# Rounds of a top-k selection and half a rotation moved between stages of a hybrid attention/SSM trunk

## The chip, the cores and the metric

One core of a Trainium2 chip runs the whole kernel in one launch. The metric is device time in microseconds (us). The engines are TensorE (matrix products), VectorE (element-wise work, DVE in the rows), ScalarE (activations, ACT), GpSimd (POOL) and SyncE, which issues most DMAs (SP). Each engine runs its own queue in order and meets the others through semaphores.

## The reference

Two layers of a streaming-encoder trunk over 512 tokens of width 1024. Each is a half-step FFN, a mixer of two parallel head groups, and another half-step FFN, with RMS norms and gates from a conditioning vector; a last norm follows. In the mixer, one projection gives queries q (8 heads of 64), one shared key k and value v, an indexer (4 heads qi, one key ki, weights wi) and the input of a state-space model (SSM). The part that matters here is the sparse attention, for each block of 128 queries:

```python
q = apply_partial_rope(q); k = ...; qi = ...; ki = ...     # rotary: t*cos + swapped(t)*sin
rel = relu(einsum('bqhd,bsd->bqhs', qi, ki))
score = einsum('bqhs,bqh->bqs', rel, wi) * idx_scale
score = where(key_chunk <= q_chunk, score, -inf)
vals, idx = top_k(score, 128)                              # topk = min(256, 512 // 4)
logits = einsum('bqhd,bqkd->bqhk', q, k[idx]) * att_scale  # -inf where vals is not finite
out = softmax(logits) @ v[idx]
```

The SSM's output passes a GELU and a gated linear unit (GLU), both groups are normed, and `w_out` projects them.

## The kernel before

Features lie on partitions, tokens along the free dimension. Every large product is split in three: an operand is a high and a low part (`w_hi`, `w_lo`, `h_hi`, `h_lo`), ScalarE makes the high part of each streamed weight tile (`split_hi`, L698), VectorE the low one (`split_lo`, L1003), and TensorE runs three matmuls (`split3`, L1706 to L1708). Each engine's order is written out by hand in its own function; there is no planner.

**The mixer.** First come twelve projection tiles, t = 0 to 11 (`project(t)` on TensorE). Between them lie rotations, the SSM's states, and, at t = 8, 9, 10, the indexer for query blocks 1, 2, 3: a product on TensorE, a rectifier on ScalarE (L873), a weighted accumulation on VectorE (`index_acc`, L1371 and L1373) into `score[b]`, whose width is 128 (b + 1): 256, 384 and 512. Block 0 needs no selection.

**Selection.** The 128 largest of each row are found in 16 rounds of 8 for each block: `topk_max` (L1385) finds the 8 largest, `topk_take` (L1391, a value load and a replacement) overwrites them with a marker. Each waits for the one before it on the same block. `topk_end` (L1396) makes the mask out of the markers.

**Head steps.** Then come 32 steps e, four blocks of eight heads. Step e: TensorE makes the logits of head e + 1 (L1990), VectorE adds the mask to those of head e and finds the row's extreme (`mask_head`, L1415), ScalarE exponentiates into `tmp_b` (`p_exps`, L888), TensorE transposes (`turn`, L2000), ScalarE copies (`p_copy`, L897), and TensorE multiplies the values of head e - 1 (L2009). Logits of e wait for the mask step of e - 2. `TOPK_WITH[e]` names the blocks whose rounds run at step e: before, blocks 1 and 2 at steps 0 to 7, blocks 2 and 3 at 8 to 15, block 3 at 16 to 23. The other rounds of block 1 are in the tiles: two beside the indexer at t = 9, four at t = 10, two at t = 11. The norm of block b - 1 runs in parts at fixed steps of block b (`att_step`, whose first part, L1425 and L1426, divides by the row sums; L903, GpSimd's L1673, L1438, L908 and L1443 follow). From step 10 TensorE also does the GLU, two tiles k at a step (`GLU_AT`), and from step 18 three matmuls at a step whose result nobody uses (`keep_streaming`, L2017). VectorE does the gate (L1531), ScalarE the tanh and the squares (L956, L963), and two splits of late weight tiles follow ScalarE's at steps 1 and 2.

**Rotations.** Eight tiles are rotated (r = 0 to 7; r = 4 to 7 are the queries, each for two heads): TensorE multiplies by a swap matrix (L1970), VectorE forms tile times cosine (L1357), swapped tile times sine (L1358) and their sum (L1359). Only the last, r = 7, is shared with GpSimd: VectorE makes the sine product at step 4 (L1527), GpSimd the cosine product (L1623) and the sum (L1626) in `last_rope`, behind the low parts of the SSM output (`y_low`, L1618). Logits of head 4 need r = 6, those of head 6 need r = 7.

Of the kernel before, what the change touches and what calls it, by code (L numbers as in the profile page):

```python
# [23 lines left out]
ALU = mybir.AluOpType  # L24
# [9 lines left out]
QB = SEQ // P  # L34
F = 2816
FT = F // P
HEADS = 8
HD = 64
AT = HEADS * HD // P
# [74 lines left out]
INDEX_FROM = 8  # L114
SUM_BEHIND = 2
KEEP_FROM = 18
TOPK_WITH = [(1, 2)] * HEADS + [(2, 3)] * HEADS + [(3,)] * HEADS + [()] * HEADS
OUT_SPLIT_AT = {0: 14, 1: 15, 19: 16, 23: 17, 25: 18, 27: 19}
PREP = {}
for m in range(4):  # L120
    for i in range(4):
        PREP[4 * m + i + 1] = (m, i)
DVE_STEPS, POOL_STEPS = 273, 86
SMALL = 72


# [65 lines left out]
def trunk(nc, a):  # L192
    ctx = ExitStack()
    with ctx:
# [3 lines left out]
        def sem(name):  # L198
            return ctx.enter_context(nc.semaphore(name))
# [176 lines left out]
        z_copy = Signal(sem("z_copy"), 12)  # L376
        swap_mm = Signal(sem("swap_mm"), 8)
        rope_done = Signal(sem("rope_done"), 8)
        last_sin = Signal(sem("last_sin"), 1)
        last_cos = Signal(sem("last_cos"), 1)  # L380
        v_tr = Signal(sem("v_tr"), 1)
        v_done = Signal(sem("v_done"), 2)
        idx_mm = Signal(sem("idx_mm"), 12)
# [308 lines left out]
        def _(act):  # L692
# [150 lines left out]
            def mixer_act(l):  # L843
# [84 lines left out]
                for t in range(12):  # L928
# [13 lines left out]
                    if t == 10:  # L942
                        for m in GELU_AT[t]:
                            gelu(m)
                act.wait_ge(*h_done.at(l, 2 * KT - 1))
                for e in range(NA):
                    b, h = e // HEADS, e % HEADS
                    p_exps(e)
                    for m in GELU_HI_AT.get(e, ()):
                        gelu_high(m)  # L950
                    if e in TANH_AT:
                        n = TANH_AT[e]
                        used(act, l, m0 + 12 + n)
                        if n >= 2:
                            act.wait_ge(*ssm_y.at(l, n - 2))
                        nc.scalar.activation(glu_t[:, n % 2, :], ps[:, 4 + n % 2, :], ACT.Tanh, scale=0.5,  # L956
                                             bias=half_bias[:, n:n + 1]).then_inc(glu_act.sem, 1)
                    if e in SQUARE_AT:
                        n = SQUARE_AT[e]
                        act.wait_ge(*ssm_y.at(l, n))  # L960
                        if n >= 2:
                            act.wait_ge(*ssm_ss.at(l, n - 2))
                        nc.scalar.activation(sq_t[:, n % 2, :], ssm_t[:, n, :], ACT.Square).then_inc(ssm_sq.sem, 1)  # L963
                    for n in SSM_HI_AT.get(e, ()):
                        act.wait_ge(*ssm_f.at(l, n))
                        nc.scalar.activation(h_hi[:, AT + n, :].rearrange("p (j t) -> p j t", t=L),
                                             ssm_t[:, n, :].rearrange("p (t j) -> p j t", t=L), ACT.Copy).then_inc(ssm_hi.sem, 1)
                    p_copy(e)
                    if e in OUT_SPLIT_AT:
                        split_hi(l, m0 + OUT_SPLIT_AT[e])  # L970
                    if b and h == 2:
                        att_square(b - 1)
                    if b and h == 7:
                        att_high(b - 1)
# [21 lines left out]
        def _(dve):  # L996
# [351 lines left out]
            def mixer_dve(l, step):  # L1348
                m0 = MIX_BASE

                def rope(r):
# [7 lines left out]
                    V.tensor_tensor(dst, part[:, 0, :], part[:, 1, :], ALU.add).then_inc(rope_done.sem, 1)  # L1359
                    dve.wait_ge(*rope_done.at(l, r))  # L1360

                def index_acc(n):

                    b, h = n // IDX_HEADS + 1, n % IDX_HEADS
                    w = (b + 1) * P
                    dve.wait_ge(*idx_relu.at(l, n))
                    if n:
                        dve.wait_ge(*idx_acc.at(l, n - 1))
                    dst, w_h = score[b], wi_n[:, b, h:h + 1]
                    if h == 0:  # L1370
                        i = V.tensor_scalar(dst, tmp_a[:, n % 2, 0:w], w_h, None, ALU.mult)  # L1371
                    else:
                        i = V.scalar_tensor_tensor(out=dst, in0=tmp_a[:, n % 2, 0:w], scalar=w_h, in1=dst, op0=ALU.mult, op1=ALU.add)  # L1373
                    i.then_inc(idx_acc.sem, 1)
# [111 lines left out]
                for t in range(2, 12):  # L1486
                    split_lo(l, m0 + t + AHEAD)
                    if t in (10, 11):
                        for _ in range(2):
                            topk_max(1)  # L1490
                            topk_take(1)
                    for r in ROPE_SLOT.get(t, ()):
                        rope(r)
                    if t == 3:
                        mask0()
                        step(V.memset(hs[:], 0.0), V.memset(dec[:, :, 0:1], 0.0))
                    if t in STATES_AT:
                        s5_scan(STATES_AT[t])
                    if INDEX_FROM <= t < INDEX_FROM + 3:
                        if t == INDEX_FROM:  # L1500
                            dve.wait_ge(*v_done.at(l, 1))
                        for n in range(IDX_HEADS):
                            index_acc((t - INDEX_FROM) * IDX_HEADS + n)
                            if t > INDEX_FROM:
                                (topk_max, topk_take)[n % 2](1)
                        topk_start(t - INDEX_FROM + 1)
                for e in range(NA):
                    b, h = e // HEADS, e % HEADS
                    blocks = TOPK_WITH[e]
                    if blocks:  # L1510
                        topk_max(blocks[0])
                    mask_head(e)
                    if len(blocks) > 1:
                        topk_max(blocks[1])
                    if blocks:
                        topk_take(blocks[0])
                    if b:
                        att_step(b - 1, h)
                    if b > 1 and h == 0:
                        att_step(b - 2, 8)  # L1520
                    if len(blocks) > 1:
                        topk_take(blocks[1])
                    if blocks and h == HEADS - 1:
                        topk_end(blocks[0])
                    if e == LAST_ROPE:
                        dve.wait_ge(*swap_mm.at(l, 7))
                        V.tensor_tensor(ssm_t[:, 1, :], ps[:, ROPE_BANKS[7][1], :], rope_s[:], ALU.mult).then_inc(last_sin.sem, 1)  # L1527
                    if e in GATE_AT:
                        n = GATE_AT[e]
                        dve.wait_ge(*glu_act.at(l, n))  # L1530
                        V.scalar_tensor_tensor(out=ssm_t[:, n, :], in0=glu_t[:, n % 2, :], scalar=1.0,  # L1531
                                               in1=u_t[:, n].rearrange("p a b -> p (a b)"), op0=ALU.add, op1=ALU.mult).then_inc(ssm_y.sem, 1)
                    if e - 1 in OUT_SPLIT_AT:
                        split_lo(l, m0 + OUT_SPLIT_AT[e - 1])
                    if e == ROOT_AT:
                        dve.wait_ge(*ssm_ss.at(l, ST - 1))
                        rms(l, 2, 4 * SW, step)
                    for n in SSM_AT.get(e, ()):
                        if n == 0:
                            dve.wait_ge(*bcast.at(l, 2))  # L1540
                        V.scalar_tensor_tensor(out=ssm_t[:, n, :], in0=ssm_t[:, n, :], scalar=half_gain[:, n:n + 1],
                                               in1=ps[:, 6, :], op0=ALU.mult, op1=ALU.mult).then_inc(ssm_f.sem, 1)
                    for n in SSM_LO_AT.get(e, ()):
                        dve.wait_ge(*ssm_hi.at(l, n))
                        V.tensor_tensor(h_lo[:, AT + n, :].rearrange("p (j t) -> p j t", t=L),
                                        ssm_t[:, n, :].rearrange("p (t j) -> p j t", t=L),
                                        h_hi[:, AT + n, :].bitcast(F32).rearrange("p (j t) -> p j t", t=L), ALU.subtract).then_inc(mix_done.sem, 1)
# [52 lines left out]
        def _(pool):  # L1600
# [16 lines left out]
                pool.wait_ge(*y_hi.at(l, m))  # L1617
                Q.tensor_tensor(h_lo[:, AT + m, :], u_t[:, m].rearrange("p a b -> p (a b)"), h_hi[:, AT + m, :].bitcast(F32), ALU.subtract).then_inc(y_done.sem, 1)  # L1618

            def last_rope(l):  # L1620

                pool.wait_ge(*z_copy.at(l, ROPE_TILE[7]))
                Q.tensor_tensor(ssm_t[:, 0, :], z_t[:, ROPE_TILE[7] % 2, :], rope_c[:], ALU.mult).then_inc(last_cos.sem, 1)  # L1623
                pool.wait_ge(*last_cos.at(l, 0))
                pool.wait_ge(*last_sin.at(l, 0))
                Q.tensor_tensor(q_t[:, AT - 1, :], ssm_t[:, 0, :], ssm_t[:, 1, :], ALU.add).then_inc(rope_done.sem, 1)  # L1626

            def ready(l, event, step):

# [38 lines left out]
            for l in range(DEPTH):  # L1668
# [14 lines left out]
                Q.memset(toep[:, 3], 0.0).then_inc(toep0.sem, 1)  # L1683
                s5_rot(l, step)
                power(l, 1)
                for m in range(ST):
                    y_low(l, m)
                last_rope(l)
                for b in range(2):
                    att_power(b)  # L1690
                power(l, 2)
# [485 lines left out]
```

## Time and profile before

| | us |
|---|---|
| median of 3 runs | 2104.31 (2103.47 to 2107.48) |
| the profiled execution | 2102.22 |
| its span | 2100.4 |
| TensorE busy | 2023.8 (96%) |
| VectorE busy | 1317.9 (63%) |
| ScalarE busy | 693.9 (33%) |
| GpSimd busy | 260.1 (12%) |

The span runs from the first to the last instruction of one profiled execution. Busy time is a sum over stages with different limits, so a stage has to be read by itself: the head steps of layer 0 lie between about 550 and 652 us, those of layer 1 between about 1574 and 1676.

### The profile page before, as it was taken

To read this page: it belongs to the slowest core of one execution; us is meant where nothing else is said; L and a number is where in the kernel's file an instruction comes from. 1 tells how busy PE (TensorE), PEld (TensorE's weight loads), DVE (VectorE), ACT (ScalarE), POOL (GpSimd) and SP (SyncE) were. 2 spreads that over 40 slices of the span, in tenths; PEclk is the share of its full clock that TensorE was granted. 3 is DMA by queue.
4 is the path that set the end of the run, shared out by engine and by line. 5 is a ranking of instruction groups with operands and counts; after the bars stand their busy time and mean duration, and the time that the engine had idled before them with its cause. 6 is when DMAs were issued, how large, how long until landed. Compare 5 with 4: busy or idle time off the path is not lost.

```text
span 2100.4 us, 25289 instructions
## 1 busy us (share of the span) xinstructions
PE 2023.8 (96%) x9548; PEld 1632.4 (78%) x9548; DVE 1317.9 (63%) x2057; ACT 693.9 (33%) x1061; POOL 260.1 (12%) x231
## 2 busy tenths in 40 slices
PE   6999899999899999999999999999998999999998
PEld 5788678877577788888878877888775787888886
DVE  6778856566884764543467697375779656545334
ACT  4332222341444422222342322233334534223223
POOL 0006900400100000000000295040001000000000
PEclk8999999999799999999999999999997999999999
DMA  8465556343101454433347365444320135463332
GB/s 290 124 212 186 157 155 183 86 109 94 56 20 52 135 172 145 158 103 92 89 139 222 121 185 152 152 146 112 100 70 22 41 89 172 120 193 115 104 93 78
DMA packets 395985, 264.77 MB, mean 126 GB/s; under 512 B 56560, under 2 KB 371672, under 8 KB 395864
## 3 DMA queue, kind: packets, MB, share of 16 engines
q1 hardware_dynamic: 387360, 260.94, 41.1%
q10 hardware_dynamic: 8504, 2.22, 0.5%
q8 instruction: 76, 1.25, 0.2%
q14 instruction: 45, 0.37, 0.1%
HBM read 254.98 MB, written 6.29 MB: 124 GB/s over the span
## 4 chain that ended last, share of the span: by engine, by line
PE 65%; issue 21%; DVE 9%; ACT 3%; DMA 1%; SPq 0%; POOL 0%; ACTq 0%; DVEq 0%; POOLq 0%
PE ps L1706 19%; PE ps L1707 18%; PE ps L1708 18%; DVE w_lo L1003 2%; DVE mod_acc L1024 2%; PE ps L1990 2%; PE ps L2009 1%; DVE h_lo L1084 1%; PE ps L1934 1%; PE ps L2017 1%; PE ps L2000 1%; PE ps L2082 1%; DMA stage<-in_ffn_w 1%; PE ps L2087 1%; PE ps L1970 1%
## 5 line engine op out<-in xcount | busy, mean ns | idle before, releaser
L1706 PE MATMUL ps<-h_hi,w_hi 128*128 128x512 f32 x1728 | 686.0, 397 | 22.1 <-DVE w_lo L1003 19.3
L1707 PE MATMUL ps<-h_lo,w_hi 128*128 128x512 f32 x1728 | 677.7, 392 | 0.0
L1708 PE MATMUL ps<-h_hi,w_lo 128*128 128x512 f32 x1728 | 677.1, 392 | 0.0
L1003 DVE TENSOR_TENSOR w_lo<-stage,w_hi 128x1024 fp32r<-128x1024 f32 (+2 forms) x322 | 394.1, 1246 | 164.4 <-ACT w_hi L698 162.1
L1706 PEld LDWEIGHTS ps<-h_hi,w_hi 128*128 128x128 f32 x1728 | 327.1, 189 | 103.7 <-DVE w_lo L1003 21.9
L1708 PEld LDWEIGHTS ps<-h_hi,w_lo 128*128 128x128 f32 x1728 | 327.1, 189 | 69.7
L1707 PEld LDWEIGHTS ps<-h_lo,w_hi 128*128 128x128 f32 x1728 | 327.0, 189 | 65.5 <-issue 0.5
L698 ACT ACTIVATE w_hi<-stage 128x1024 fp32r<-128x1024 f32 (+2 forms) x322 | 318.9, 1016 | 172.3 <-PE ps L1708 165.1
L1706 PE MATMUL ps<-g_hi,w_hi 128*128 128x512 f32 x704 | 276.7, 393 | 1.1 <-DVE g_lo L1318 1.1
L1707 PE MATMUL ps<-g_lo,w_hi 128*128 128x512 f32 x704 | 274.2, 389 | 0.0
L1708 PE MATMUL ps<-g_hi,w_lo 128*128 128x512 f32 x704 | 274.2, 389 | 0.0
L817 ACT ACTIVATE tmp_a<-ps 128x512 f32<-128x512 f32 x84 | 50.2, 597 | 494.9 <-PE ps L1708 494.8
L1316 DVE TENSOR_TENSOR tmp_b<-tmp_a,ps 128x512 f32<-128x512 f32 x84 | 57.5, 684 | 244.5 <-ACT tmp_a L817 242.2
L1024 DVE SCALAR_TENSOR_TENSOR mod_acc<-mod_stage,c_silu,mod_acc 128x1024 f32<-128x1024 f32 x126 | 187.2, 1485 | 8.5
L1109 DVE SCALAR_TENSOR_TENSOR x<-ps,gate,x 128x512 f32<-128x512 f32 x112 | 84.0, 750 | 152.8 <-PE ps L1708 152.8
L1706 PEld LDWEIGHTS ps<-g_hi,w_hi 128*128 128x128 f32 x704 | 132.2, 188 | 30.4 <-DVE g_lo L1318 1.8
L1708 PEld LDWEIGHTS ps<-g_hi,w_lo 128*128 128x128 f32 x704 | 132.1, 188 | 27.9
L1707 PEld LDWEIGHTS ps<-g_lo,w_hi 128*128 128x128 f32 x704 | 132.2, 188 | 26.8
L1606 POOL TENSOR_TENSOR small<-small 128x4 f32<-128x4 f32 x9 | 12.9, 1437 | 976.2 <-DVE small L1043 976.2
L821 ACT ACTIVATE g_hi<-tmp_b 128x512 fp32r<-128x512 f32 x88 | 55.6, 632 | 173.8 <-DVE tmp_b L1316 170.2
L1318 DVE TENSOR_TENSOR g_lo<-tmp_b,g_hi 128x512 fp32r<-128x512 f32 x84 | 67.8, 807 | 58.9 <-ACT g_hi L821 58.9
L1990 PE MATMUL ps<-k_t,q_t 64*128 64x128 f32 (+3 forms) x128 | 58.3, 550 | 3.2 <-POOL q_t L1626 3.2
(304 smaller groups left out, 1790.6 us busy)
## 6 DMA issues: line engine op xcount, KB each, us to landing
stage<-in_ffn_w SPq DMA_DIRECT2D x210, 512.0 KB, 4.7
mod_stage<-in_mod_w SPq DMA_DIRECT2D x144, 512.0 KB, 5.6
stage<-in_ffn_w SPq DMA_DIRECT2D x64, 448.0 KB, 4.0
stage<-in_w_in SPq DMA_DIRECT2D x20, 512.0 KB, 3.8
mod_first<-in_mod_w SPq DMA_DIRECT2D x16, 512.0 KB, 9.4
stage<-in_w_out SPq DMA_DIRECT2D x16, 512.0 KB, 4.1
x_in<-in_x SPq DMA_DIRECT2D x4, 512.0 KB, 5.1
stage<-in_w_in SPq DMA_DIRECT2D x8, 256.0 KB, 3.7
```

Of the source, the lines that this page charges most:

```text
L698: nc.scalar.activation(w_hi[:, c % RING, 0:n], stage[:, c % RING, 0:n], ACT.Copy).then_inc(w_split_hi.sem, 1)
L817: nc.scalar.activation(tmp_a[:, f % 2, :], ps[:, 2 * (f % 2), :], ACT.Silu).then_inc(silu_done.sem, 1)
L821: nc.scalar.activation(g_hi[:, f - FIRST_TILE[p], :], tmp_b[:, f % 2, :], ACT.Copy).then_inc(g_hi_done.sem, 1)
L1003: V.tensor_tensor(w_lo[:, c % RING, 0:n], stage[:, c % RING, 0:n], w_hi[:, c % RING, 0:n].bitcast(F32), ALU.subtract).then_inc(w_split_lo. ...
L1024: i = V.scalar_tensor_tensor(out=mod_acc[:], in0=chunk, scalar=c_silu[:, k:k + 1], in1=mod_acc[:], op0=ALU.mult, op1=ALU.add)
L1109: V.scalar_tensor_tensor(out=x[:, n, :], in0=ps[:, bank, :], scalar=gate[:, k3, n:n + 1], in1=x[:, n, :], op0=ALU.mult, op1=ALU.add).then_ ...
L1316: V.tensor_tensor(tmp_b[:, f % 2, :], tmp_a[:, f % 2, :], ps[:, 2 * (f % 2) + 1, :], ALU.mult).then_inc(g_full.sem, 1)
L1318: V.tensor_tensor(g_lo[:, f - FIRST_TILE[p], :], tmp_b[:, f % 2, :], g_hi[:, f - FIRST_TILE[p], :].bitcast(F32), ALU.subtract).then_inc(g_ ...
L1706: mm(out, hi, rhs_hi, start=first, stop=False)
L1707: mm(out, hi, rhs_lo, start=False, stop=False)
L1708: return mm(out, lo, rhs_hi, start=False, stop=last)
L1990: mm(ps[:, e % 2, 0:(b + 1) * P], q_t[r, h // 2, b * P:(b + 1) * P], k_t[r, 0:(b + 1) * P], start=True, stop=True).then_inc(logit.sem, 1)
```

## The change

Three rounds of block 1 leave steps 5 to 7 for t = 11, ahead of the rotation there. Three rounds of block 3 leave steps 13 to 15 for steps 16 to 18, which then have two each. Rotation 6 is divided as rotation 7 was: VectorE keeps the sine product, GpSimd makes the cosine product into `tmp_b` and adds. Since the exponentials write `tmp_b` too, ScalarE waits for that addition before step 0.

```diff
-TOPK_WITH = [(1, 2)] * HEADS + [(2, 3)] * HEADS + [(3,)] * HEADS + [()] * HEADS
+TOPK_WITH = [(1, 2)] * 5 + [(2,)] * 3 + [(2, 3)] * 5 + [(2,)] * 3 + [(3,)] * HEADS + [()] * HEADS
+TOPK_MORE = (16, 17, 18)
...
                 act.wait_ge(*h_done.at(l, 2 * KT - 1))
+                act.wait_ge(*rope_done.at(l, 6))
                 for e in range(NA):
...
+                def rope_sin(r):
+                    dve.wait_ge(*swap_mm.at(l, r))
+                    if r == 7:
+                        dve.wait_ge(*rope_done.at(l, 6))
+                    V.tensor_tensor((tmp_b if r == 6 else ssm_t)[:, 1, :], ps[:, ROPE_BANKS[r][1], :], rope_s[:], ALU.mult).then_inc(last_sin.sem, 1)
...
                     if t in (10, 11):
-                        for _ in range(2):
+                        for _ in range(2 if t == 10 else 5):
                             topk_max(1)
                             topk_take(1)
                     for r in ROPE_SLOT.get(t, ()):
-                        rope(r)
+                        (rope if r < 6 else rope_sin)(r)
...
                     if len(blocks) > 1:
                         topk_take(blocks[1])
-                    if blocks and h == HEADS - 1:
-                        topk_end(blocks[0])
+                    if e in TOPK_MORE:
+                        topk_max(3)
+                        topk_take(3)
+                    if h == HEADS - 1 and b + 1 < QB:
+                        topk_end(b + 1)
                     if e == LAST_ROPE:
-                        dve.wait_ge(*swap_mm.at(l, 7))
-                        V.tensor_tensor(ssm_t[:, 1, :], ps[:, ROPE_BANKS[7][1], :], rope_s[:], ALU.mult).then_inc(last_sin.sem, 1)
+                        rope_sin(7)
...
+            def rope_add(l, r):
+                pool.wait_ge(*z_copy.at(l, ROPE_TILE[r]))
+                pool.wait_ge(*rope_done.at(l, r - 1))
+                part = tmp_b if r == 6 else ssm_t
+                Q.tensor_tensor(part[:, 0, :], z_t[:, ROPE_TILE[r] % 2, :], rope_c[:], ALU.mult).then_inc(last_cos.sem, 1)
+                pool.wait_ge(*last_cos.at(l, r - 6))
+                pool.wait_ge(*last_sin.at(l, r - 6))
+                Q.tensor_tensor(q_t[:, r - 4, :], part[:, 0, :], part[:, 1, :], ALU.add).then_inc(rope_done.sem, 1)
...
                 power(l, 1)
+                rope_add(l, 6)
                 for m in range(ST):
                     y_low(l, m)
-                last_rope(l)
+                rope_add(l, 7)
```

## Rows read from the trace of the kernel before

**Rows 1.** Windows of layer 0's head steps: blocks 0, 1 and 2.

```profile
core 0: us, PE busy (x) PEld busy (x) DVE busy (x) ACT busy (x) POOL busy (x), PEclk, DMA share, GB/s
550.00:571.00 21.00, 13.43 (x43) 8.91 (x42) 20.18 (x73) 9.74 (x31) 8.37 (x6) 0.61 0.23 70
571.00:597.00 26.00, 24.50 (x103) 17.27 (x102) 24.47 (x74) 9.59 (x30) 0.56 (x1) 0.79 0.00 1
597.00:621.00 24.00, 24.00 (x140) 18.17 (x140) 19.68 (x51) 12.73 (x32) 1.95 (x2) 1.00 0.08 23
```

**Rows 2.** TensorE's waits, 577 to 640 us, all: total us, times, longest.

```profile
PE ps L2009 <- DVE ki_t L1426: 0.7, 1, 0.7
```

**Rows 3.** Timeline of VectorE, last projection tile: start, length, instruction, [idle before].

```profile
547.53 0.69 DVE L1003 TENSOR_TENSOR w_lo<-stage,w_hi 128x512 fp32r<-128x512 f32 x1 [1.21 <-ACT w_hi L698]
548.14 0.42 DVE L1385 MAX8 small<-score 128x8 f32<-128x256 f32 x1
...
549.34 0.43 DVE L1385 MAX8 small<-score 128x8 f32<-128x256 f32 x1
...
550.32 0.68 DVE L1357 TENSOR_TENSOR tmp_b<-z_t,rope_c 128x512 f32<-128x512 f32 x1
550.92 0.68 DVE L1358 TENSOR_TENSOR tmp_b<-ps,rope_s 128x512 f32<-128x512 f32 x1
...
552.50 0.43 DVE L1385 MAX8 small<-score 128x8 f32<-128x256 f32 x1 [0.17 <-DVE q_t L1359]
```

**Rows 4.** Timeline of VectorE, split of tile 14 and step 4.

```profile
556.75 0.69 DVE L1003 TENSOR_TENSOR w_lo<-stage,w_hi 128x512 fp32r<-128x512 f32 x1 [0.32 <-ACT w_hi L698]
...
562.19 0.41 DVE L1385 MAX8 small<-score 128x8 f32<-128x256 f32 x1
562.52 0.27 DVE L1415 CUSTOM_DVE_ANT_0 tmp_a<-ps,score 128x128 f32<-128x128 f32 x1
...
563.20 0.07 DVE L1391 MATCH_VALUE_LOAD score<-small,score 128x8 f32 x1
...
563.58 0.07 DVE L1391 MATCH_VALUE_LOAD score<-small,score 128x8 f32 x1
...
564.11 0.68 DVE L1527 TENSOR_TENSOR ssm_t<-ps,rope_s 128x512 f32<-128x512 f32 x1
```

**Rows 5.** Timeline of GpSimd, the sum of rotation 7.

```profile
564.93 1.26 POOL L1626 TENSOR_TENSOR q_t<-ssm_t 128x512 f32<-128x512 f32 x1 [2.23 <-DVE ssm_t L1527]
```

**Rows 6.** Timeline of ScalarE, last rectifier and first exponential's table load.

```profile
543.91 0.60 ACT L873 ACTIVATE tmp_a<-ps 128x512 f32<-128x512 f32 x1 [0.16 <-DVE score L1373]
...
553.21 1.28 ACT L888 ACT_TABLE_LOAD   x1 [3.31 <-DVE small L1415]
```

**Rows 7.** Timeline of TensorE: logits of 6 and 8, first GLU matmul, turn 19.

```profile
566.34 0.77 PE L1990 MATMUL ps<-k_t,q_t 64*128 64x128 f32 x2 [1.58 <-POOL q_t L1626]
...
569.22 1.22 PE L1990 MATMUL ps<-k_t,q_t 64*128 64x256 f32 x2
...
578.82 0.79 PE L1706 MATMUL ps<-h_hi,w_hi 128*128 128x512 f32 x1
...
609.80 0.49 PE L2000 MATMUL ps<-ident,tmp_b 128*128 128x128 f32 x3
```

**Rows 8.** Timeline of VectorE, the mask of step 8 and parts of step 16.

```profile
571.55 0.41 DVE L1415 CUSTOM_DVE_ANT_0 tmp_a<-ps,score 128x256 f32<-128x256 f32 x1
...
596.79 0.68 DVE L1385 MAX8 small<-score 128x8 f32<-128x512 f32 x1
597.39 0.53 DVE L1415 CUSTOM_DVE_ANT_0 tmp_a<-ps,score 128x384 f32<-128x384 f32 x1
...
597.93 0.67 DVE L1391 MATCH_REPLACE8 score<-small,score 128x512 f32<-128x512 f32 x1
```

**Rows 9.** Timeline of VectorE, two indexer accumulations and the split of tile 15.

```profile
542.34 0.49 DVE L1371 TENSOR_SCALAR score<-tmp_a,wi_n 128x512 f32<-128x512 f32 x1
...
543.08 0.73 DVE L1373 SCALAR_TENSOR_TENSOR score<-tmp_a,wi_n,score 128x512 f32<-128x512 f32 x1
...
559.28 1.06 DVE L1003 TENSOR_TENSOR w_lo<-stage,w_hi 128x512 fp32r<-128x512 f32 x1
```

More of the change, by code:

```diff
@@ L122 @@
         PREP[4 * m + i + 1] = (m, i)
-DVE_STEPS, POOL_STEPS = 273, 86
+DVE_STEPS, POOL_STEPS = 271, 86
 SMALL = 72
@@ L378, in trunk @@
         rope_done = Signal(sem("rope_done"), 8)
-        last_sin = Signal(sem("last_sin"), 1)
-        last_cos = Signal(sem("last_cos"), 1)
+        last_sin = Signal(sem("last_sin"), 2)
+        last_cos = Signal(sem("last_cos"), 2)
         v_tr = Signal(sem("v_tr"), 1)
@@ L1618, in y_low @@
                 Q.tensor_tensor(h_lo[:, AT + m, :], u_t[:, m].rearrange("p a b -> p (a b)"), h_hi[:, AT + m, :].bitcast(F32), ALU.subtract).then_inc(y_done.sem, 1)
[L1620 to L1626, printed above, removed]
+            def rope_add(l, r):
[6 more added lines that the diff above has]
+                Q.tensor_tensor(q_t[:, r - 4, :], part[:, 0, :], part[:, 1, :], ALU.add).then_inc(rope_done.sem, 1)
             def ready(l, event, step):
```

## The prediction

> **What bounds the kernel now.** The page's engine table shows TensorE busiest by far, but the change touches only some 70 us of each layer, so I read that stretch by windows [rows 1]. It has three regimes. In the first (heads 0 to 7 of attention block 0) VectorE is busy 20.18 of 21.00 us and TensorE 13.43. In the second (block 1) both are near full. In the third (block 2) TensorE is busy 24.00 of 24.00 and VectorE 19.68. The waits settle who sets the pace: from 577 to 640 us TensorE waits once, 0.7 us, at its start [rows 2]. It runs head steps, GLU matmuls and streaming matmuls end to end, so **from step 10 TensorE is the bound**, and whatever VectorE saves or spends there counts only where a turn (transpose) of probabilities comes late. Before step 10 VectorE sets the pace, helped by ScalarE's exponentials. I work the sum in layer 0 and double it: layer 1 shows the same waits and durations, moved by 1023.9 us.
>
> **The change, part by part.** All times of layer 0.
>
> *Last projection tile.* VectorE gets the split of tile 13 at 547.53, after a wait on ScalarE, and then runs two rounds of block 1. Alone, a round is a chain: 548.14 to 549.34 is 1.20 us [rows 3], because each half needs the other's result. They ended just as the swapped tile for rotation 6 was there, so their slot is full already. Three rounds more cost 3 x 1.20 = 3.6 us, with no idle time to take them. The rotation shrinks from three operations (550.32 to 552.50, with a short wait: 2.18 us) to one, 0.60 from start to start (the step from its first operation to its second). So step 0 begins at 552.50 + 3.6 - 1.58 = 554.52, **+2.0 us**.
>
> *The new wait on ScalarE.* The exponentials write the scratch in which GpSimd now adds rotation 6, so head 0's exponential, its table load and everything behind them on ScalarE wait for that addition: the two high parts of the SSM output, the probability copy and the split of tile 14, for which VectorE waits, and TensorE's first turn. VectorE's sine product would end at 553.92 + 0.68 = 554.60; GpSimd starts 0.14 after such an end and takes 1.27 (564.11 + 0.68 to 564.93) [rows 4, 5], and who waits for it starts 0.14 after its end (TensorE, 566.34 [rows 7]): ScalarE at 556.15, where it began its table load at 553.21 [rows 6]. ScalarE is **2.9 us** late. VectorE, 2.0 late, meets it at the split of tile 14 (0.32 idle today [rows 4]) and is 2.9 late from there to step 5. The cosine product costs nothing on this path: it needs only tile 10 and rotation 5, there by 542.3, and GpSimd has nothing to do then.
>
> *Steps 5 to 7* lose block 1's round. A step with both blocks is 1.92 (562.19 to 564.11 [rows 4]), of which block 1 is 0.33 from its maximum to the mask and 0.38 from its load to the other's (563.20 to 563.58), 0.72 unrounded. The full gain would be 2.2, but the remaining block's round is a chain of about 1.5 (0.55 maximum, 0.14 gap, mask beside it, 0.07 load, 0.54 replace, 0.13), so at most 3 x 0.43 = 1.3 is there. It also meets the other ring: head 6 waits for rotation 7 on GpSimd (1.58 on TensorE [rows 7]), 2.9 late like all of it; then TensorE, at its lower clock, needs logits, turn and values twice. Carried on from its rows: logits of 6 at 569.28, of 7 at 570.70, of 8 at 572.16, ready 1.22 + 0.22 later, at 573.60. Head 8's mask stood at 571.55 [rows 8]. **Net at block 1's start +2.05**; VectorE's own chain would give +1.7, no catching up +2.9. Steps 8 to 12 are unchanged and carry the delay into the GLU at step 10 (578.82 [rows 7]), where TensorE is the bound and it can't be made up.
>
> *Steps 13 to 15* lose block 3's round, 0.60 for the maximum (596.79 to 597.39) and 0.67 for the replacement [rows 8], 1.27 us each on VectorE. I count that as 0 for the time: TensorE waits there neither for VectorE nor for an exponential [rows 2]. It only builds a lead, and the lead is cut: step 16's last part waits for block 0's high part, made after TensorE's turn of 15 (to 597.8).
>
> *Steps 16 to 18* each get a second round of block 3, in chain with the first. By 0.69 + 0.14 + 0.08 + 0.68 + 0.13 a 512-wide round is 1.7 us. In the frame of before: step 16 ends at 600.06, step 17 masks at 600.8 and ends at 604.9 with its division and gate, step 18 masks at 605.5 and ends at 608.5, step 19 masks at 609.3. Exponential 18 just makes its turn; 19 ends at 610.6, and its turn stood at 609.80 [rows 7]. **+0.8** (0 if VectorE packs tighter by half a microsecond a step, 1.5 if looser). Steps 20 to 23 have slack to take the rest, with TensorE pacing.
>
> *A collision on GpSimd.* The cosine product would run from about 542.45 to 543.7, beside the second indexer accumulation of block 3. Today such a meeting shows once: the 512-wide split at 559.28 took 1.06 beside GpSimd's low parts, against 0.69 at 547.53 [rows 3, 9], so 0.37 more. The accumulation at 543.08 releases ScalarE's last rectifier at 543.91 [rows 6, 9], and behind that stand the GELU and the split for which VectorE waits until 547.53. Bounds: 0, if they don't meet, and 0.63, if it waits for GpSimd's end. I take **+0.4**, by the one such meeting in the trace.
>
> The Trainium skill ("SBUF — State Buffer", on the physical ports) says that GpSimd and a VectorE operation with two SBUF inputs hold one port pair exclusively, whoever is first, for the whole instruction. The split's 1.06 us beside GpSimd [rows 9] agrees in kind; the rule's own result here is rival E, and by it the total would be 1.2 us higher than by the row.
>
> **Sum.** Per layer 2.05 + 0.8 + 0.4 = 3.25; two layers 6.5, rounded with the unrounded 0.84 to 6.6. The profiled execution took 2102.22 us (span 2100.4), so it would be 2108.8. The median before is 2104.31, 2.1 above it; on that, **2110.9 us**, +0.31%. Less than 0.2% (4.2 us) a measurement of this kernel can't tell from no change.
>
> **Rivals.**
> *A, VectorE paces everything up to step 16.* Then removed rounds give their whole length: +2.0 - 3 x 0.72 - 3 x 1.27 = -3.95 a layer, and the added rounds lie under TensorE: 2104.31 - 7.9 = 2096.4. For it: VectorE is busy 24.47 of 26.00 in block 1 [rows 1]. Against it: TensorE has no wait after the one at 576.66 [rows 2]. It decides from the point where turns 13 to 16 would start earlier than GLU matmuls allow.
> *B, the clock comes back sooner.* TensorE's granted clock is 0.61 on average in block 0 and 0.79 in block 1 [rows 1]: it falls to the 1.2 GHz level in the idle time before step 0, and 0.79 over 26 us is 10.9 us at half, so it is back at 2.4 GHz at 581.9. The GLU begins at 578.82 [rows 7], so 3.1 us of it run at half, worth 1.5. With lighter steps 5 to 7 TensorE idles less ahead of it; if the clock were back by then, and steps 16 to 18 were free: 2.05 + 0.4 - 1.5 = 0.95 a layer, 2106.2.
> *C, only block 0 costs.* Lead absorbs steps 16 to 18, no collision: 2 x 2.05, 2108.4, on the very edge of what can be told.
> *D, nothing is absorbed.* ScalarE's 2.9 stays, 0.84, and the upper 0.63: 4.4 a layer, 2113.1.
> *E, the accumulation waits out the whole cosine product.* The one-input operation ahead of it (542.34 to 542.83 [rows 9]) makes GpSimd wait first; GpSimd then runs 1.27, to 544.1, and the accumulation starts 1.0 late: 2.05 + 0.84 + 1.0 = 3.9 a layer, 2112.1. For it: 1.06 at 559.28 could be such a wait. Against: GpSimd's place in time is unknown by some tenths. (It is the skill's rule above.)
>
> **How the numbers follow.** Forecast 0.40, E 0.12, D 0.10, C 0.19, B 0.13, A 0.06. A is faster. B lies within 0.2%, C is split, two thirds within, and a little of the forecast's spread falls below 2108.5: same 0.30. Slower 0.64. The range leaves out A, the low part of B and what exceeds D by a microsecond: 2105.5 to 2114.0. The likeliest case's own range is 2109 to 2113.
>
> **What would show it.** In the changed profile: five rounds 1.20 apart after the tile-13 split, the first exponential's table load 2.9 us later against that split and released by GpSimd; the steps 5 to 7 at about 1.5 us with a wait on the logits of 6; the GLU 2 us later against the last projection matmul; after it TensorE without waits until turn 19, which waits some 0.8 us for ScalarE; the same GLU pace at steps 13 to 15. The forecast is wrong if step 0's exponential is not late, if turns 13 to 16 close up, or if the granted clock rises before the first GLU matmul.

## The result, and the profile after

| us | before | changed |
|---|---|---|
| median | 2105.79 (2103.47 to 2107.48, 4 runs) | 2124.7 (2119.12 to 2127.95, 4 runs) |
| the profiled execution | 2102.22 | 2119.12 |
| its span | 2100.4 | 2117.3 |
| mean granted clock over the span | 0.978 | 0.972 |

The ratio is 1.0096, with a 95% interval of 1.0083 to 1.0109: 0.96% slower (by the two medians of the table 0.90%), where 0.31% was forecast, and outside the range given (2105.5 to 2114.0). The sign was right and the size was a third of what came.

The two kernels have the same number of matmuls (9548), so the n-th of one can be set against the n-th of the other. What follows is the start after less the start before, counted from the last projection matmul of tile 10, at five places, in us:

| shift at | turn 0 | first GLU matmul | logits of 13 | turn 19 | turn 24 and the mixer's end |
|---|---|---|---|---|---|
| layer 0 | +3.59 | +2.72 | +3.45 | +4.13 | +5.77 |
| layer 1 | +3.58 | +2.12 | +2.47 | +3.19 | +12.75 |

With -0.58 ahead of layer 0's stretch and -1.05 between the mixers (the kernel before has two short stretches at half clock there, at 1268 and at 1480; the changed kernel has one, at 1258) that is 5.77 + 12.76 - 1.63 = 16.9, the difference of the spans. Up to turn 19 the forecast holds; behind it, most of all in layer 1, it doesn't.

The same windows of layer 0 as in [rows 1]. In the third TensorE now has idle time (23.46 of 24.00) and the granted clock is no longer 1.00:

```profile
core 0: us, PE busy (x) PEld busy (x) DVE busy (x) ACT busy (x) POOL busy (x), PEclk, DMA share, GB/s
550.00:571.00 21.00, 9.87 (x29) 6.62 (x30) 17.99 (x65) 8.60 (x26) 9.65 (x7) 0.62 0.24 73
571.00:597.00 26.00, 25.27 (x99) 17.84 (x99) 22.81 (x71) 10.01 (x33) 0.56 (x1) 0.72 0.00 1
597.00:621.00 24.00, 23.46 (x120) 17.22 (x120) 20.18 (x50) 11.92 (x30) 0.94 (x1) 0.93 0.08 23
```

TensorE's waits (in the rows: total us, times, longest), 577 to 640 us, against [rows 2]: the old one is there, and one new:

```profile
PE ps L2023 <- DVE ki_t L1435: 0.7, 1, 0.7
PE ps L2014 <- ACT tmp_b L889: 0.5, 1, 0.5
```

VectorE's last projection tile, against [rows 3] and the accumulations of [rows 9]. The first row is an accumulation that took 1.43 us. Of the five rounds the maxima are shown; they lie 1.20 to 1.21 apart. Then come the sine product and step 0:

```profile
542.50 1.43 DVE L1382 SCALAR_TENSOR_TENSOR score<-tmp_a,wi_n,score 128x512 f32<-128x512 f32 x1
...
547.64 0.69 DVE L1005 TENSOR_TENSOR w_lo<-stage,w_hi 128x512 fp32r<-128x512 f32 x1 [1.20 <-ACT w_hi L699]
548.25 0.42 DVE L1394 MAX8 small<-score 128x8 f32<-128x256 f32 x1
...
549.45 0.43 DVE L1394 MAX8 small<-score 128x8 f32<-128x256 f32 x1
...
550.66 0.43 DVE L1394 MAX8 small<-score 128x8 f32<-128x256 f32 x1
...
551.87 0.43 DVE L1394 MAX8 small<-score 128x8 f32<-128x256 f32 x1
...
553.07 0.43 DVE L1394 MAX8 small<-score 128x8 f32<-128x256 f32 x1
...
554.05 0.68 DVE L1369 TENSOR_TENSOR tmp_b<-ps,rope_s 128x512 f32<-128x512 f32 x1
554.65 0.42 DVE L1394 MAX8 small<-score 128x8 f32<-128x256 f32 x1
```

GpSimd's two halves of rotation 6, against [rows 5], and ScalarE's table load, against [rows 6]: it now waits for GpSimd and begins at 556.22.

```profile
541.88 1.50 POOL L1636 TENSOR_TENSOR tmp_b<-z_t,rope_c 128x512 f32<-128x512 f32 x1 [97.97 <-DVE q_t L1361]
554.88 1.27 POOL L1639 TENSOR_TENSOR q_t<-tmp_b 128x512 f32<-128x512 f32 x1 [11.50 <-DVE tmp_b L1369]
```
```profile
556.22 1.28 ACT L889 ACT_TABLE_LOAD   x1 [6.90 <-POOL q_t L1639]
```

TensorE's logits of 6, first GLU matmul and turn 19, against [rows 7], with what follows the turn. The streaming matmuls (L2031) took 0.97 us for three ahead of the wait and 1.53 behind it:

```profile
569.36 0.76 PE L2004 MATMUL ps<-k_t,q_t 64*128 64x128 f32 x2 [1.58 <-POOL q_t L1639]
...
580.96 0.79 PE L1720 MATMUL ps<-h_hi,w_hi 128*128 128x512 f32 x1
...
611.85 0.97 PE L2031 MATMUL ps<-w_hi 128*128 128x512 f32 x3
613.35 0.55 PE L2014 MATMUL ps<-ident,tmp_b 128*128 128x128 f32 x3 [0.54 <-ACT tmp_b L889]
...
616.18 1.53 PE L2031 MATMUL ps<-w_hi 128*128 128x512 f32 x3
```

Layer 1 has the same wait of 0.54, ahead of its turn 19 at 1641.05. Its windows behind that show where the time went. TensorE has no idle time from 1643 to 1667, but from about 1644 to 1664 it runs at 0.50, the 1.2 GHz level. The kernel before stays at 1.00 (2.4 GHz) from 1608 to 1666.

```profile
1643.00:1645.00 2.00, 2.00 (x6) 1.16 (x6) 2.00 (x4) 1.18 (x4) 0.00 (x0) 0.69 0.01 4
1645.00:1650.00 5.00, 5.00 (x18) 3.60 (x17) 3.08 (x10) 1.08 (x3) 0.00 (x0) 0.50 0.37 108
1650.00:1660.00 10.00, 10.00 (x36) 7.89 (x35) 3.50 (x9) 2.16 (x6) 1.02 (x1) 0.50 0.00 0
...
1663.00:1665.00 2.00, 2.00 (x14) 1.83 (x12) 0.00 (x0) 0.96 (x2) 0.00 (x0) 0.69 0.00 0
1665.00:1667.00 2.00, 2.00 (x10) 1.13 (x9) 0.97 (x2) 1.70 (x4) 0.00 (x0) 1.00 0.00 0
```

In layer 0 the time at half clock is shorter, some 3.5 us (0.58 in the window 616 to 618, 0.56 in 618 to 620, 1.00 from 620). So the theory to test: **the wait ahead of turn 19 is as long as forecast, and its price is the clock behind it.** The rival: block 3's rounds delay VectorE in steps 16 to 23 and hold TensorE by something else.

### The profile page after: what moved, and what is told of

The parts are those of the page before. It is cut to its first block, busy times and chain, and to the rows that moved or that the text cites. A ratio compares the mean times of both kernels' runs of the same rounds, so it can differ in the third digit from the quotient of the medians.

```text
span 2117.3 us, 25297 instructions
## 1 busy us (share of the span) xinstructions
PE 2034.7 (96%) x9548; PEld 1639.7 (77%) x9548; DVE 1320.1 (62%) x2053; ACT 694.0 (33%) x1061; POOL 266.6 (13%) x235
## 3 DMA queue, kind: packets, MB, share of 16 engines
q8 instruction: 76, 1.25, 0.2%
## 4 chain that ended last, share of the span: by engine, by line
PE 62%; issue 22%; DVE 11%; ACT 3%; DMA 1%; ACTq 0%; POOL 0%; SPq 0%; DVEq 0%; POOLq 0%
PE ps L1720 18%; PE ps L1721 17%; PE ps L1722 17%; DVE mod_acc L1026 2%; DVE w_lo L1005 2%; PE ps L2004 1%; PE ps L2023 1%; DVE h_lo L1086 1%; DVE small L1394 1%; PE ps L2031 1%; DVE score L1400 1%; PE ps L2096 1%; DMA stage<-in_ffn_w 1%; PE ps L1948 1%; PE ps L2101 1%
```

## The experiments

The kernel before had a median of 2103.19 beside the first four, 2103.13 beside the next four, 2103.29 beside the ninth and tenth, 2103.48 and 2102.85 beside the last two.

**1. Block 3's rounds alone.** The kernel before, with only these lines of the change:

```diff
+TOPK_WITH = [(1, 2)] * HEADS + [(2, 3)] * 5 + [(2,)] * 3 + [(3,)] * HEADS + [()] * HEADS
+TOPK_MORE = (16, 17, 18)
```

> The kernel before with only block 3's three rounds moved from steps 13-15 to 16-18. Theory (the clock): VectorE is late with the mask of step 19, TensorE waits some 0.5 us before turn 19, and that wait costs it the 2.4 GHz clock for a while: per layer 0.9 for the wait and 1.5 to 9.3 for the clock, so 2110 to 2126 us against 2105.8, and the granted clock at 0.50 somewhere in steps 19 to 24 of at least one layer. Rival (the late first turn): the clock loss comes from the longer idle time ahead of step 0, which this kernel does not have: only the wait itself, 2105.8 + 1.8 = 2107.6 us, clock 1.00 from step 16 on.

Measured: 2117.22 (2105.76 to 2122.28), ratio 1.0058 [1.004, 1.0076]. It reads like the changed kernel: the same wait, and then half clock, in layer 1 for 23 us (0.50 from 1638 to 1661).

```profile
611.13 0.55 PE L2004 MATMUL ps<-ident,tmp_b 128*128 128x128 f32 x3 [0.54 <-ACT tmp_b L889]
```
```profile
614.00:616.00 2.00, 2.00 (x7) 1.60 (x7) 2.00 (x6) 0.27 (x1) 0.00 (x0) 0.50 0.00 0
616.00:618.00 2.00, 2.00 (x10) 1.53 (x8) 1.36 (x2) 1.08 (x3) 0.00 (x0) 0.65 0.84 252
...
1640.00:1660.00 20.00, 20.00 (x64) 14.50 (x63) 7.10 (x20) 3.80 (x11) 1.02 (x1) 0.50 0.09 27
```

Turn 19 is 1.24 and 0.60 late; turn 24 is 2.87 and 11.79. Three moved rounds alone cost 14 us.

**2. The change without block 3's part.**

```diff
-TOPK_WITH = [(1, 2)] * 5 + [(2,)] * 3 + [(2, 3)] * 5 + [(2,)] * 3 + [(3,)] * HEADS + [()] * HEADS
-TOPK_MORE = (16, 17, 18)
+TOPK_WITH = [(1, 2)] * 5 + [(2,)] * 3 + [(2, 3)] * HEADS + [(3,)] * HEADS + [()] * HEADS
+TOPK_MORE = ()
```

> The changed kernel with block 3's rounds back in steps 13-15. Theory (the clock): no wait before turn 19, the clock stays at 1.00 from the second GLU step on; what is left is 0.7 us (collision with the cosine product) and 2.05 us (steps 0 to 9) a layer: 2105.8 + 5.5 = 2111.3 us. Rival (the late first turn causes the clock loss): 2117 to 2126 us, clock at 0.50 after step 18 as in the changed kernel.

Measured: 2109.68 (2108.39 to 2114.47), ratio 1.003 [1.0017, 1.0043]: +6.5. The GLU starts 2.70 and 2.71 late, the mixer ends 3.29 and 3.12 late, there is no wait from 580 to 640, and the clock stays at 1.00. Experiments 1 and 2 add up to 20.5, near the 18.9 of the whole.

**3. The wait filled.** The whole change, with four streaming matmuls more ahead of turn 19, which have no result that anybody uses:

```diff
-                        keep_streaming(3, m0 + (15 if e < 24 else 16))
+                        keep_streaming(7 if e == 19 else 3, m0 + (15 if e < 24 else 16))
```

> The changed kernel with seven streaming matmuls instead of three at step 19, so that TensorE works through the time in which it waited for exponential 19. Theory (the idle time costs the clock): the clock stays at 1.00 through steps 19 to 24; the wait's length stays: 2105.8 + 2 x (2.75 + 1.0) = 2113.3 us. Rival (the clock falls for another reason, the late first turn or what VectorE does): as the changed kernel, 2119 to 2128 us.

Measured: 2110.81 (2109.73 to 2112.67), ratio 1.0033 [1.0021, 1.0045]: +7.6. Adding work took 14 us off the changed kernel's median, or 11 if each is set against the kernel before that ran beside it. The turn comes no less late than in the changed kernel, without idle time ahead of it, and the clock is kept (windows behind the timeline):

```profile
611.04 1.89 PE L2031 MATMUL ps<-w_hi 128*128 128x512 f32 x7
612.76 0.49 PE L2014 MATMUL ps<-ident,tmp_b 128*128 128x128 f32 x3
```
```profile
613.00:616.00 3.00, 3.00 (x21) 2.35 (x20) 3.00 (x8) 2.55 (x5) 0.49 (x1) 1.00 0.00 0
616.00:621.00 5.00, 5.00 (x36) 4.08 (x35) 4.79 (x14) 2.28 (x6) 0.05 (x1) 1.00 0.35 105
```

That settles the theory against the rival: VectorE's work is the same, turn 19 is as late or later (+0.92 from steps 13 to 19, where the changed kernel has 0.68 and 0.72), and the clock's price is gone. But the edit does two things at once: it takes the idle time away and puts four wide matmuls in. Whether the first or the second keeps the clock it can't tell.

**4. Rotation 6 shared, no round moved.**

```diff
-TOPK_WITH = [(1, 2)] * 5 + [(2,)] * 3 + [(2, 3)] * 5 + [(2,)] * 3 + [(3,)] * HEADS + [()] * HEADS
+TOPK_WITH = [(1, 2)] * HEADS + [(2, 3)] * HEADS + [(3,)] * HEADS + [()] * HEADS
...
-                        for _ in range(2 if t == 10 else 5):
+                        for _ in range(2):
```

> The kernel before with only rotation 6 shared with GpSimd, all top-k rounds as before. By the working of the prediction VectorE begins step 0 earlier by 1.6 - 0.7, but ScalarE waits for GpSimd's sum: sine ends at 551.7, sum 551.8 to 553.1, table load at 553.2 as before. Net 0: 2105.8 +- 1 us. Rival: GpSimd's part costs by itself (slower sum, a longer collision): over 2108 us.

Measured: 2103.74, ratio 1.0001 [0.9992, 1.001]; turn 0 stands 0.03 and 0.04 earlier. The 1.6 us that VectorE saves go to ScalarE's wait and the collision.

**5. The same through a scratch of its own.** Rotation 6 uses `ssm_t[:, 2:4]` instead of `tmp_b`, ScalarE waits for nothing, and the cosine product comes behind the last accumulation:

```diff
-                act.wait_ge(*rope_done.at(l, 6))
...
-                part = tmp_b if r == 6 else ssm_t
+                part = ssm_t[:, 2:4] if r == 6 else ssm_t[:, 0:2]
+                if r == 6:
+                    pool.wait_ge(*idx_acc.at(l, 11))
...
```

Both products of rotation 6 also wait until the SSM is done with these tiles.

> The top-k rounds as before; rotation 6 shared with GpSimd through two tiles of ssm_t that nothing else uses then, so that ScalarE needs no wait, and GpSimd's cosine product behind the last indexer accumulation, so that it meets none of them. Theory: VectorE begins step 0 1.6 us earlier, ScalarE's table load follows, and steps 0 to 9 carry 1.6 a layer into the GLU: 2103.2 - 3.2 = 2100.0 us. Rival (steps 0 to 9 are set by TensorE's and GpSimd's part, not by VectorE's start): no gain, 2103.2.

Measured: 2104.05 (2099.58 to 2105.02), ratio 1.0 [0.9991, 1.0009]. A miss: turn 0 came 1.60 and 1.59 earlier and the GLU 1.42 and 1.59, as expected, and yet the logits of 13 stood at -0.73 in layer 0 and +0.93 in layer 1. The GLU starts at half clock in all kernels up to here, and in layer 1 the clock came back one step later. TensorE in this kernel, layer 1:

```profile
1602.54 0.79 PE L1728 MATMUL ps<-h_hi,w_hi 128*128 128x512 f32 x1
...
1606.57 1.22 PE L2012 MATMUL ps<-k_t,q_t 64*128 64x256 f32 x2
1607.72 0.79 PE L1728 MATMUL ps<-h_hi,w_hi 128*128 128x512 f32 x1
```

and in the kernel before, where the second GLU tile follows at full clock:

```profile
1602.69 0.79 PE L1706 MATMUL ps<-h_hi,w_hi 128*128 128x512 f32 x1
...
1606.37 0.70 PE L1990 MATMUL ps<-k_t,q_t 64*128 64x256 f32 x2
1607.00 0.51 PE L1706 MATMUL ps<-h_hi,w_hi 128*128 128x512 f32 x1
```

**6. Block 1's rounds moved on top of 5**, `for _ in range(2 if t == 10 else 5)` and `[(1, 2)] * 5 + [(2,)] * 3`. **7. Block 1's rounds moved alone**, rotation 6 left on VectorE.

> As the kernel with its own scratch for rotation 6, and block 1's three rounds moved from steps 5-7 to the last projection tile. Against the changed kernel without block 3's move (+6.5 us measured) it lacks ScalarE's wait (0.9 a layer by the prediction) and the collision (0.7 a layer). Theory: step 0 begins 2.0 late, 1.1 a layer is left at the GLU: 2103.2 + 2.2 = 2105.4 us. Rival (the wait on ScalarE costs nothing, because VectorE is late anyway): 2103.2 + 4.1 = 2107.3.

Measured: 2104.71 (2102.19 to 2111.7), ratio 1.0014 [1.0004, 1.0025]. Turn 0 is 2.02 late and the GLU 1.14 and 1.13. In layer 0 the clock came back later (0.50 until 591, where the kernel before is at 1.00 from 582), and the mixer ended 3.85 late; in layer 1, where it did not, 0.73.

> The kernel before with only block 1's three rounds moved from steps 5-7 to the last projection tile; rotation 6 stays whole on VectorE. Theory: step 0 begins 3.6 late, steps 5 to 7 give back 1.2 to 1.6: 2.2 a layer, 2103.2 + 4.4 = 2107.6 us. Rival (rounds are worth the same wherever they stand, 0.72 against 0.72): 2103.2.

Measured: 2110.08, ratio 1.0032 [1.002, 1.0043]. Turn 0 is 3.62 late: as late as with the shared rotation of the change, so the sharing through `tmp_b` bought nothing. With a scratch of its own (experiment 6 against 7) the sharing bought 1.6 at turn 0, 1.6 to 1.7 at the GLU and 5.4 us of the median, with no clock held. The GLU is 2.81 and 2.72 late, the logits of 13 by 5.27 and 5.05: the clock came back later in both layers.

**8. An idle stretch without lateness.** The kernel before, with the three streaming matmuls of step 19 taken out:

```diff
-                        keep_streaming(3, m0 + (15 if e < 24 else 16))
+                        keep_streaming(0 if e == 19 else 3, m0 + (15 if e < 24 else 16))
```

> The kernel before without the three streaming matmuls of step 19, nothing else changed: nothing is late, but TensorE stands idle for some 0.4 us ahead of turn 19, as long as it waited there in the changed kernel. Theory (the idle time costs the clock): granted clock 0.50 after step 19 in at least one layer, and 1.5 to 10 us a layer: 2105 to 2120 us with a wide spread. Rival (the clock falls because of lateness or the load of VectorE): 2102.5 to 2103.2 us, clock 1.00.

Measured: 2102.39 (2101.14 to 2107.46), ratio 0.9999 [0.999, 1.0008]. Half a miss. TensorE idles 0.38 us ahead of turn 19 in both layers. The clock fell in layer 0 (windows below), where the mixer then ended 2.68 late, and not in layer 1:

```profile
613.00:616.00 3.00, 3.00 (x13) 2.60 (x12) 2.85 (x7) 1.17 (x4) 0.00 (x0) 0.53 0.36 107
616.00:621.00 5.00, 5.00 (x21) 3.41 (x21) 1.91 (x6) 0.68 (x4) 0.00 (x0) 0.60 0.14 41
...
1640.00:1645.00 5.00, 5.00 (x33) 4.02 (x33) 4.73 (x12) 2.00 (x6) 0.00 (x0) 1.00 0.37 110
```

An idle stretch here is a chance of losing the clock, not a fixed price. This edit too changes two things: there is idle time, and there are three wide matmuls fewer.

**9 and 10. The clock held in steps 0 to 9.** Streaming matmuls in TensorE's idle time, on the kernel before and on experiment 5 (there with 10 ahead of turn 0):

```diff
+WARM = {0: 14, 1: 3, 2: 3, 4: 3, 5: 3, 6: 3, 7: 3, 8: 5, 9: 5}
...
+                    if e == 5:
+                        keep_streaming(5, m0 + 12)
...
+                    if e in WARM:
+                        keep_streaming(WARM[e], m0 + 12)
```

> The kernel before with streaming matmuls (whose result nobody uses) put in TensorE's idle time of steps 0 to 9: 14 ahead of turn 0, 3 to 5 ahead of the turns 1, 2 and 4 to 9, 5 ahead of the logits of 6. Theory (the granted clock follows how long TensorE stands idle, and the GLU's first steps run at 1.2 GHz because of the idle time in steps 0 to 6): the clock is 1.00 from the first GLU matmul on in both layers, no matmul starts of the GLU lie 0.43 us apart, and the GLU's stretch is 1.2 to 1.6 us a layer shorter: 2103.1 - 2.8 = about 2100.3. Rival (the added matmuls, in order ahead of the turns, delay them, and VectorE sets the pace before step 10 in any case): the clock rises, but logits and turns come later by what the matmuls take, 0.5 to 2 us a layer: 2103 to 2107. Second rival (matmuls added to so thin a mix do not bring the clock back): 4 of the slow GLU starts stay, 2103.

Measured: 2101.1 (2098.57 to 2104.2), ratio 0.9989 [0.998, 0.9998]. In layer 0 the clock is 1.00 all along and the logits of 13 stand 2.68 earlier. In layer 1 it fell once (0.88 in the window 1574 to 1595, 0.63 in 1595 to 1602), and the mixer ended 1.24 late, though TensorE's idle stretches ahead are as long as in layer 0 (1.07 ahead of turn 0, 1.25 ahead of the logits of 6).

> The same streaming matmuls (10 ahead of turn 0) on top of the kernel in which rotation 6 is divided through a scratch of its own and no round is moved, which started step 0 1.6 us earlier a layer and ended where the kernel before did. Theory (that gain was taken back by the clock's later return in the GLU): with the clock held, both stay: 1.6 + 1.3 a layer, 2103.1 - 5.8 = about 2097.3. Rival (streaming matmuls delay the turns): the 1.6 stays gone, 2102 to 2105.

Measured: **2096.5** (2094.55 to 2099.37), ratio 0.9968 [0.9956, 0.998], the fastest of all: -4.14 in layer 0, -4.36 in layer 1. Here is the first window of [rows 1], now at 1.00 where the kernel before had 0.61, and the stretch of the GLU's start:

```profile
550.00:571.00 21.00, 18.24 (x81) 11.91 (x80) 20.54 (x76) 10.50 (x33) 9.69 (x7) 1.00 0.22 66
571.00:578.00 7.00, 6.47 (x34) 4.74 (x32) 6.97 (x22) 2.19 (x7) 0.00 (x0) 1.00 0.00 0
578.00:584.00 6.00, 6.00 (x31) 4.52 (x31) 6.00 (x20) 3.21 (x10) 0.56 (x1) 1.00 0.00 0
```

So the gain that experiment 5 lost is there when the clock holds. Layer 0, where both kernels keep it, puts the own scratch at 4.14 - 2.68 = 1.46.

**11 and 12. The whole change with the clock held.** Experiment 3 with the lines of 9; then with 30 instead of 14 ahead of turn 0.

> The changed kernel with seven instead of three streaming matmuls at step 19 and with the streaming matmuls of steps 0 to 9 that took the kernel before to 2101.1. The clock is at 2.4 GHz all along then, so this is the change's price without the clock. Theory (the prediction's terms are waits on VectorE, ScalarE and GpSimd and don't hang on the clock): 2.05 at block 1's start, 0.7 for the collision, 0.8 to 1.3 at turn 19, 3.6 to 4.0 a layer above 2101.1, about 2108.5. Rival (a good part of the 2.05 came from logits, turn and values at the lower clock in steps 6 and 7, where the fewer rounds can be made up once TensorE is quick): 2.0 to 3.0 a layer, 2105.1 to 2107.1.

Measured: 2112.95 (2109.16 to 2114.78), ratio 1.0041 [1.0027, 1.0054], above both expected values. The change makes turn 0 later, so the fourteen ended long ahead of it and the clock fell; at half clock the added matmuls were in the way (logits of 8 at +7.83 and +6.70):

```profile
560.72 0.47 PE L2015 MATMUL ps<-ident,tmp_b 128*128 128x128 f32 x1 [4.67 <-ACT tmp_b L890]
```

That the added matmuls were in the way is argued from experiment 12, where the logits of 8 are at +3.91.

> As the kernel before it (the whole change, seven streaming matmuls at step 19, streaming matmuls in steps 0 to 9), with 30 instead of 14 ahead of turn 0. There the fourteen ended 4.67 us ahead of the turn, which the change makes later, and the granted clock fell to 0.50 at about 560; with rotation and rounds as before the same fourteen ended 1.08 us ahead and it stayed at 1.00. Theory: thirty end about 1.0 us ahead of the turn, the clock stays at 1.00 in both layers, and what is left above 2101.1 is the change's waits alone: 3.6 to 4.0 a layer by the measured terms, 2108.5, or less, down to 2105, if TensorE at full clock makes up part of them in steps 5 to 9. Rival (the fourteen weren't the reason, the added matmuls are what is late in steps 5 to 9): 2112 to 2114 again.

Measured: 2106.51 (2102.66 to 2112.56), ratio 1.0019 [1.001, 1.0027]. The clock is 1.00 in both layers of the profiled execution, and the idle time ahead of turn 0 is that of experiment 9 again:

```profile
558.32 0.33 PE L2015 MATMUL ps<-ident,tmp_b 128*128 128x128 f32 x1 [1.07 <-ACT tmp_b L890]
```

Against the kernel before, the mixer ended 1.23 and 1.17 late. Experiment 9's layer 0, with the clock held as well, ended 2.68 early. So the change's waits alone cost 1.23 + 2.68 = 3.91 a layer: 2.98 by the logits of 13 and 0.92 at turn 19. The medians differ by less, 5.4 instead of 7.8, and experiment 9's own lost clock in one layer is 3.9 of its profiled time. The profile of 12 is also one of its two fastest executions (2102.85, mean clock 0.992); the other ten had 0.986 to 0.989, so the clock was probably held less well in them.

## Why the prediction was wrong

By its own steps:

- **Last projection tile, +2.0 at step 0:** right. Split to step 0's maximum is 547.64 to 554.65, 7.01, against 4.97 before: +2.04. With ScalarE's wait taken out, turn 0 is 2.02 late (experiment 6).
- **The wait on ScalarE, +2.9:** right. Split to table load is 8.58 against 5.68: +2.90. With the collision's 0.69 that is turn 0's 3.59.
- **Net +2.05 at block 1's start:** right. The GLU starts 2.70 late in experiments 2 and 3; less 0.69 that is 2.01. Head 8's mask in the changed kernel, at 573.67 against 571.55, says the same: 2.12, with the 0.58 ahead 2.70.
- **The collision, +0.4:** too small by 0.3. The accumulation at 542.50 took 1.43 instead of the 0.73 of [rows 9]. It was stretched by 0.70, so it ended 0.69 late. Rival E had the kind right and the size too large. It let GpSimd wait for the end of the one-input operation ahead (here 542.25); that would put the accumulation's end at 542.25 + 1.27 + 0.73 = 544.25, and it came at 543.93. GpSimd began at 541.88, and 541.88 + 1.27 + 0.73 = 543.88 is near it. But the product itself took 1.50 and ended at 543.38, so it was held up as well, and a part of such a wait isn't excluded. The Trainium skill's port pair rule ("SBUF — State Buffer", section "SBUF: two separate sides") has the later of the two wait for the whole of the other. The accumulation agrees in kind; by the product's recorded end it would have ended at 544.11, 0.18 later than it did.
- **Steps 13 to 15, 0:** right; the shift moves by 0.02 from the logits of 13 to turn 16.
- **Steps 16 to 18, "+0.8":** the step that failed. Turn 19 is 0.68 and 0.72 later than the steps before it, so the wait was sized right and its price was not. I charged the delay alone. Behind it TensorE's clock stood at 1.2 GHz for 3.5 us in layer 0 and 20 us in layer 1, worth 5.77 - 4.13 = 1.6 and 12.75 - 3.19 = 9.6. Experiment 1 shows that these rounds alone do it. Experiment 3 shows that lateness is not the cause: with the wait filled by wide matmuls, the clock's price is gone.
- **The clock at the GLU's start:** rival B took it as a possible gain only. In the runs it went either way: +0.73 and +0.35 in the changed kernel, +2.5 and +2.3 in experiment 7, -1.4 in experiment 9's layer 0. The forecast had no term for it. In layer 1 of the changed kernel the clock was even back at 1.00 from 1596 to 1599, ahead of the first GLU matmul, which is one of the forecast's own signs of being wrong; it then fell again until 1613.

The sum for the profiled execution is then 2.03 + 0.69 + 0.73 + 0.68 + 1.64 = 5.77 for layer 0. Rivals A (2096.4), B, C and D each fail on that: nothing closed up in steps 13 to 16, and more than block 0 cost. D came nearest, for the wrong reason: it let the whole 2.9 stand, and 0.9 of it was made up.

I read "TensorE without waits" [rows 2] as slack on the other engines, and not as a state that could be lost.

Idle time alone does not lose it, though. Half a microsecond behind the window of [rows 2], at turn 28, TensorE in the kernel before waits for longer than the changed kernel does at turn 19, and keeps the clock:

```profile
638.90 0.96 PE L2017 MATMUL ps<-w_hi 128*128 128x512 f32 x3
640.53 0.66 PE L2000 MATMUL ps<-ident,tmp_b 128*128 128x128 f32 x4 [0.67 <-ACT tmp_b L888]
641.02 1.00 PE L2009 MATMUL ps<-v_n,qi_t 128*128 128x64 f32 x8
641.96 1.12 PE L1990 MATMUL ps<-k_t,q_t 64*128 64x512 f32 x2
```
```profile
640.00:643.00 3.00, 2.47 (x14) 1.65 (x14) 3.00 (x4) 1.07 (x3) 0.00 (x0) 1.00 0.23 59
```

Every kernel here has this wait, 0.66 to 0.68 us in both layers, and none of these 28 waits was followed by half clock. What stands around the wait differs: behind turn 19 come eight column sums, one column wide, and logits 384 wide, behind turn 28 no such sums, and logits 512 wide. No run here varies that alone. So what is shown is the price of a wait in this place, among these matmuls; whether those have a share in it is not shown.

The Trainium skill ("TensorE: Matmul & The Clock Gate", section "HAM oscillation — how this bites in real kernels") tells of a kernel in which every wait for data throws the clock back to half rate. The 0.54 us ahead of turn 19 agree in kind, though the waits of that kernel are several times as long; the 0.67 us ahead of turn 28 do not.

What stays open: why the clock came back in 3.5 us in layer 0 and in 20 us in layer 1 behind equal waits (the engine was busy throughout in both), why 0.38 us of idle time cost it in one layer of experiment 8 and not in the other, and why turn 28's wait never cost it. The median of the changed kernel is also 5.6 above its profiled execution; the other three executions had a mean granted clock of 0.967 to 0.970 against 0.972, so more of the same is likely, but their stretches were not recorded.

## What to carry to other kernels

Where a long stretch of small matmuls runs at full clock, a new wait on TensorE can cost far more than its length by what the clock does behind it (here 1.6 to 11.2 us for 0.54 us), and it need not (0.67 us at turn 28 cost no clock). Read the granted clock behind each wait before pricing a new one. Before moving work towards such a stretch, see which turn has no lead left, and try to fill the idle time with matmuls that need nothing, sized to the wait: too few (14 where 30 were needed) bought nothing (2112.95 against 2110.81 without any in steps 0 to 9). A scratch buffer shared with an engine that comes next can give back all that a shared operation saves: 1.6 us a layer here, kept only by a buffer of its own. Against the kernel before, that gain showed in the time only once the clock was held.

## What the runs showed of the hardware that was not expected

- An idle stretch of 0.54 us ahead of turn 19, in a run of turns, values, logits and column sums, was followed by a granted clock of 0.50 for 3.5 to 23 us in four of four cases (the changed kernel and experiment 1), though TensorE was busy throughout behind it. One of 0.38 us cost the clock in one of two layers. One of 0.67 us ahead of turn 28 cost it in none of 28 cases.
- Idle stretches of 1.07 us ahead of turn 0 and 1.25 us ahead of the logits of 6, with streaming matmuls near them, were passed at 1.00 in experiment 9's layer 0 and in both layers of experiment 12. In experiment 9's layer 1, with the same stretches, the clock fell behind the second.
- Three streaming matmuls took 0.97 us at full clock and 1.53 to 1.65 at half.
- A GpSimd product with two SBUF inputs that began first stretched a VectorE accumulation from 0.73 to 1.43 us, and took 1.50 us itself, where the same product behind the accumulations took 1.29 (experiment 5). The same came in both layers of experiments 2, 3 and 4.
